# The last chunk of expert weights by halves of its output columns, in a one-core decoder layer with 32 experts

## What is computed

```python
h = h + mixed @ w_out
h = h + MoE(RMSNorm(h))      # top-4 of 32 experts, at most a few tokens each
output = RMSNorm(h)          # [1, 256, 1024] float32

# one expert, for the tokens that chose it
hu  = xb @ w_up[e] + b_up[e]                       # 1024 -> 2 x 1024
act = min(hu[:, :1024], 7) * sigmoid(1.702 * ...) * (clip(hu[:, 1024:], -7, 7) + 1)
y   = act @ w_down[e] + b_down[e]                  # 1024 -> 1024
# each token's outputs are weighted by its gates and added to its row of h
```

## Time and profile before

| | |
|---|---|
| time, median of 3 runs | 1242.39 us (1242.19 to 1242.48) |
| time of the profiled execution | 1243.28 us |
| its span, first to last instruction | 1241.6 us |
| TensorE busy | 1160.3 us, 93% |
| VectorE, ScalarE busy | 392.5 us (32%), 241.3 us (19%) |
| read from memory | 455.35 MB, 368 GB/s over the span |
| granted TensorE clock, mean | 0.982 |

### The profile page before, as it was taken

The page is one execution under the profiler, slowest core; times in us unless marked ns, Lnnn a source line. Parts: engine busy times, 40 slices in busy tenths (PEclk is TensorE's granted clock), DMA queues, the critical chain, the costliest instruction groups (busy, mean ns, idle before and its releaser), DMA issues.

```text
span 1241.6 us, 16246 instructions
## 1 busy us (share of the span) xinstructions
PE 1160.3 (93%) x6984; PEld 593.1 (48%) x6984; DVE 392.5 (32%) x670; ACT 241.3 (19%) x334; POOL 10.8 (1%) x29
## 2 busy tenths in 40 slices
PE   9999999999999999988898889989898988989997
PEld 8888887888633334333333333333333333333332
DVE  7765746666522112121111111112121112111112
ACT  5343445554401001010000000000000001000002
POOL 2000000000000000000000000000000000000000
PEclk9999999999999999999999999999999999999999
DMA  8744333496999999999999999999999999999996
GB/s 263 260 170 179 136 136 136 153 362 227 364 423 425 433 431 430 430 432 431 433 431 433 429 435 431 432 434 430 433 430 435 430 433 434 429 433 429 425 427 276
DMA packets 46429, 456.95 MB, mean 368 GB/s; under 512 B 5588, under 2 KB 5736, under 8 KB 31128
## 3 DMA queue, kind: packets, MB, share of 16 engines
q1 hardware_dynamic: 46088, 455.61, 88.2%
q10 hardware_dynamic: 304, 0.79, 0.2%
HBM read 455.35 MB, written 1.05 MB: 368 GB/s over the span
## 4 chain that ended last, share of the span: by engine, by line
PE 59%; DMA 36%; DVE 3%; ACT 1%; issue 0%; SPq 0%; DVEq 0%
PE ps L1410 57%; DMA ring<-in_w_up_dram 22%; DMA arena<-in_w_up_dram 10%; DMA ring<-in_w_down_dram 3%; DMA ring<-in_w_in_dram 1%; PE ps L1924 1%; DVE w_split L910 1%; ACT w_split L627 0%; PE ps L1815 0%; PE ps L1604 0%; DVE arena L955 0%; DVE arena L1077 0%; PE ps L1712 0%; DVE bias_p L954 0%; DVE arena L956 0%
## 5 line engine op out<-in xcount | busy, mean ns | idle before, releaser
L1410 PE MATMUL ps<-ring,arena 128*64 128x512 f32 x2304 | 521.4, 606 | 51.9 <-DMA ring<-in_w_up_dram 50.4
L1410 PEld LDWEIGHTS ps<-ring,arena 128*64 128x64 f32 x2304 | 163.5, 139 | 379.5 <-issue 301.0
L1410 PE MATMUL ps<-arena 128*64 128x512 f32 (+3 forms) x920 | 202.8, 563 | 18.2 <-DMA arena<-in_w_up_dram 17.3
L1329 DVE TENSOR_SCALAR arena<-ps 128x512 f32<-128x512 f32 x32 | 22.1, 692 | 487.1 <-PE ps L1410 487.1
L1410 PEld LDWEIGHTS ps<-arena 128*64 128x64 f32 (+1 forms) x920 | 77.9, 148 | 130.1 <-issue 99.5
L910 DVE TENSOR_TENSOR w_split<-ring,w_split 128x2048 fp32r<-128x2048 f32 x48 | 109.9, 2291 | 82.0 <-ACT w_split L627 81.8
L820 ACT ACTIVATE arena<-arena 128x512 f32<-128x512 f32 x32 | 20.2, 631 | 551.9 <-DVE arena L1329 551.9
L1410 PE MATMUL ps<-w_split,x_split 128*128 128x512 f32 x528 | 123.4, 392 | 1.0 <-DVE w_split L910 0.6
L627 ACT ACTIVATE w_split<-ring 128x2048 fp32r<-128x2048 f32 x47 | 89.8, 1914 | 111.4 <-PE ps L1410 95.7
L1410 PEld LDWEIGHTS ps<-w_split,x_split 128*128 128x128 f32 x528 | 98.4, 188 | 22.0 <-issue 1.2
L1410 PE MATMUL ps<-x_split,w_split 128*128 128x256 f32 (+1 forms) x544 | 93.0, 331 | 0.0
(11 more groups left out here) (245 smaller groups left out, 603.1 us busy)
## 6 DMA issues: line engine op xcount, KB each, us to landing
ring<-in_w_up_dram SPq DMA_DIRECT2D x38, 4096.0 KB, 31.1
ring<-in_w_down_dram SPq DMA_DIRECT2D x19, 4096.0 KB, 30.0
arena<-in_w_up_dram SPq DMA_DIRECT2D x12, 4096.0 KB, 31.1
ring<-in_w_up_dram SPq DMA_DIRECT2D x20, 2048.0 KB, 11.9
ring<-in_w_in_dram SPq DMA_DIRECT2D x17, 2048.0 KB, 7.9
arena<-in_w_down_dram SPq DMA_DIRECT2D x7, 4096.0 KB, 29.9
arena<-in_w_up_dram SPq DMA_DIRECT2D x8, 2048.0 KB, 15.8
ring<-in_w_down_dram SPq DMA_DIRECT2D x8, 2048.0 KB, 24.3
```

The lines of the kernel that those rows point to most:

```text
L1329: dve.tensor_scalar(glu_c, ps[bank][:, :], LIMIT, None, ALU.min).then_inc(glu_ok, 1)
L1410: return pe.matmul(dst, lhsT, rhs, start=start, stop=stop, skip_group_check=True)
```

## The change

It has four parts.

1. F is loaded by output columns: first columns 0 to 511 of all four rows (1 MB), then columns 512 to 1023 of rows 0 and 1, of row 2, and of row 3. The rows that are copied per partition are then 2 KB long each.
2. TensorE multiplies F half by half: four products for half 0, then k0 and k1 of half 1, then `last_share` of half 0, then k2 and k3 of half 1, then `last_share` of half 1. E is taken as two groups of rows, half 0 before half 1 in each. The two halves use two banks (`LAST_BANK`), and each is evicted to `y_last` by itself, 64 partitions by 512. The 31st expert's `scatter` moves from behind F to between E and F.
3. The final norm squares, weights and sums 128 x 512 pieces: four squares instead of two, the first columns' squares folded into a bias (`ssq`) for the square root, and all four output pieces are weighted by `lnf` first and scaled by the inverse root later.
4. U2, U3, G0 and G1 are loaded in two pieces of 1 MB each, and TensorE may begin on the first.

The pieces stand in the order of the engines: SyncE, ScalarE, VectorE, TensorE.

```diff
+                    at_once = 1 if u == 2 and c >= 2 else 2
+                    sp.dma_start(dst[:, 0:at_once, :], rows[:, 2 * (c % 2):2 * (c % 2) + at_once, :]).then_inc(landed, 16)
+                    if at_once == 1:
+                        sp.dma_start(dst[:, 1, :], rows[:, 2 * (c % 2) + 1, :]).then_inc(part_in[c - 2], 16)
...
+                        sp.dma_start(dst[:, 0:2, :], rows[:, 0:2, :]).then_inc(chunk_in[place], 16)
+                        sp.dma_start(dst[:, 2:4, :], rows[:, 2:4, :]).then_inc(part_in[2 + d], 16)
...
-                for lo, hi, landed in pieces:
-                    sp.dma_start(dst[:, lo:hi, :], rows[:, lo:hi, :]).then_inc(landed, 16)
-                if d:
-                    for half, landed in enumerate((last_part_in, last_half_in)):
-                        cols = slice(half * 512, half * 512 + 512)
-                        sp.dma_start(dst[:, 3, cols], rows[:, 3, cols]).then_inc(landed, 16)
...
+            sp.dma_start(dst[:, :, 0:512], rows[1, :, :, 0:512]).then_inc(early_in[3], 16)
+            sp.dma_start(dst[:, 0:2, 512:D], rows[1, :, 0:2, 512:D]).then_inc(chunk_in[PLACES - 1], 16)
+            sp.dma_start(dst[:, 2, 512:D], rows[1, :, 2, 512:D]).then_inc(last_part_in, 16)
+            sp.dma_start(dst[:, 3, 512:D], rows[1, :, 3, 512:D]).then_inc(last_half_in, 16)
...
-            act.activation(y_last[:, 0, :], ps[1][:, :], ACT.Copy, scale=g_slot[:, 1:2]).then_inc(y_out, 1)
+            def last_part(half):
+                rows = slice(half * CAP, half * CAP + CAP)
+                act.wait_ge(half_sum, half + 1)
+                act.activation(y_last[rows, 0, :], ps[LAST_BANK[half]][rows, :], ACT.Copy, scale=g_slot[rows, 1:2])\
+                   .then_inc(y_out, 1)
+            def last_square(t, half):
+                act.wait_ge(sum_ps, 2 * half + t + 1)
+                act.activation(at(t * D + half * 512, 512), ps[SUM_BANK[2 * t + half]][:, :], ACT.Square,
+                               accum_out=ssq4[:, t, half:half + 1]).then_inc(last_sq, 1)
...
+            last_part(0)
+            last_square(0, 0)
+            last_part(1)
+            act.wait_ge(scaled_ok, 1)
+            last_square(1, 0)
+            for t in range(TT):
+                if t:
+                    act.wait_ge(scaled_ok, 3)
+                last_square(t, 1)
+                act.wait_ge(part_ok, 2)
+                act.wait_ge(last_sq, 3 + t)
+                last_square_root(t)
...
+            last_low(0)
             dve.wait_ge(lnf_in, 16)
+            weighted(1, 0)
+            last_low(1)
+            dve.wait_ge(last_sq, 1)
+            weighted(0, 0)
+            dve.wait_ge(last_sq, 2)
+            dve.tensor_scalar(ssq[:, :], ssq4[:, :, 0], 1.0 / D, EPS, ALU.mult, ALU.add).then_inc(part_ok, 1)
+            weighted(1, 1)
+            dve.wait_ge(last_sq, 3)
+            weighted(0, 1)
             last_inverse(0)
+            out_half(0, 0)
             last_inverse(1)
+            out_half(0, 1)
+            out_half(1, 0)
...
+            for half in range(2):
+                last_down(0, half, (0, 1))
+            chunk_landed(last_turn, TURN_CHUNKS - DOWN_CHUNKS)
+            for half in range(2):
+                last_down(0, half, (2, 3))
             pe.wait_ge(y_ok, n_last(3))
             pe.wait_ge(selT_ok, n_last(4))
             for t in range(TT):
                 for piece in range(2):
                     scatter(0, t, piece)
-            pe.wait_ge(y_out, n_last(4))
+            pe.wait_ge(early_in[3], 16)
+            last_down(1, 0, range(4)).then_inc(half_sum, 1)
+            pe.wait_ge(chunk_in[PLACES - 1], 64)
+            last_down(1, 1, (0, 1))
             pe.wait_ge(selT_ok, n_last(5))
-            for t in range(TT):
-                last_share(0, t)
             pe.wait_ge(y_ok, n_last(4))
             for t in range(TT):
-                last_share(1, t)
+                for piece in range(2):
+                    last_share(piece, t, 0)
+            pe.wait_ge(last_part_in, 16)
+            last_down(1, 1, (2,))
+            pe.wait_ge(last_half_in, 16)
+            last_down(1, 1, (3,)).then_inc(half_sum, 1)
+            pe.wait_ge(y_out, n_last(4) + 1)
+            for t in range(TT):
+                last_share(0, t, 1)
+            pe.wait_ge(y_ok, n_last(4) + 1)
+            for t in range(TT):
+                last_share(1, t, 1)
```

More of the change, by code:

```diff
@@ L235, in layer @@
             sem(n) for n in ("last_part_in", "last_half_in", "ln1_in", "ln1_ps", "xs_ok", "glr_split_ok"))
-        first_half_in = [sem(f"first_half_in{c}") for c in range(DENSE_RING)]
+        part_in = [sem(f"part_in{c}") for c in range(DENSE_RING + 2)]
         vec_in, glr_in, bias_in, router_in, glaw_in, lnf_in = (
@@ L533, in _ @@
             end = TURN_CHUNKS - DOWN_CHUNKS
             sp.wait_ge(chunk_used, last_turn * TURN_CHUNKS + (end - PLACES + 1))
[L535 to L546 removed]
+            rows = w_down[0, E - 1, :, :].rearrange("(p d s) n -> d p s n", d=DOWN_CHUNKS, s=4)
@@ new lines, in _ @@
+            dst = chunk_at[PLACES - 2].rearrange("p (s n) -> p s n", s=4)
+            sp.dma_start(dst[:, 0:2, :], rows[0, :, 0:2, :]).then_inc(early_in[2], 16)
+            sp.dma_start(dst[:, 2:4, :], rows[0, :, 2:4, :]).then_inc(chunk_in[PLACES - 2], 16)
+            sp.wait_ge(chunk_used, last_turn * TURN_CHUNKS + (end + 1 - PLACES + 1))
+            dst = chunk_at[PLACES - 1].rearrange("p (s n) -> p s n", s=4)
+            sp.dma_start(dst[:, :, 0:512], rows[1, :, :, 0:512]).then_inc(early_in[3], 16)
@@ L1890, in first_down, with down @@
                     ins.then_inc(chunk_used, 1)
-            def down(i, u, last, bank=3, source=None, between=None, late=False, parts=False):
-                first = down_end(u, last) - DOWN_CHUNKS
-                hidden = (actT if source is None else source).rearrange("p (k s) -> p k s", k=4)
+            def down(i, u, between=None, late=False, parts=False):
+                first, bank = down_end(u, False) - DOWN_CHUNKS, 3
+                hidden = actT.rearrange("p (k s) -> p k s", k=4)
                 bias(bank, u, 2 * D)
                 pe.wait_ge(actT_ok, i * UNROLL + (u + 1))
-                if not last:
-                    chunk_landed(i, first)
+                chunk_landed(i, first)
                 for d in range(DOWN_CHUNKS):
@@ L1977, in expert_pe @@
                 else:
-                    down(i, u, False, late=bool(late), parts=by_chunk and u > 1)
+                    down(i, u, late=bool(late), parts=by_chunk and u > 1)
             pe.wait_ge(xin_half_ok, 1)
@@ L2014, in down_between @@
                     one_hot_transposed(last_turn * (TT * UNROLL) + TT * UNROLL, 0)
-            down(last_turn, UNROLL - 2, False, between=down_between, late=True)
-            down(last_turn, UNROLL - 1, True, bank=1, source=act_last)
+            down(last_turn, UNROLL - 2, between=down_between, late=True)
+            pe.wait_ge(actT_ok, n_last(4))
+            for half in range(2):
+                last_bias(half)
+            pe.wait_ge(early_in[2], 16)
+            for half in range(2):
+                last_down(0, half, (0, 1))
+            chunk_landed(last_turn, TURN_CHUNKS - DOWN_CHUNKS)
+            for half in range(2):
+                last_down(0, half, (2, 3))
             pe.wait_ge(y_ok, n_last(3))
```

113 lines of the change are left out of this document (59 added, 54 removed).

## The result

The changed kernel takes **1249.39 us**, the median of six runs (1247.68 to 1251.63), beside 1242.43 for the kernel before on the same chip; the ratio is 1.0051, with a 95% interval of 1.0040 to 1.0062. It is slower by half a per cent. The profiled execution took 1248.15 us with a span of 1246.4, so 4.8 us more than the span of 1241.6 before. The forecast was 1247.1 (1244.5 to 1249.2), and for the profiled execution 1248.0 with a span near 1246.3. The profiled execution fits to 0.2 us; the median lies 2.3 above the forecast and 0.2 above the range.

A forecast was written before the change was run, and what follows sets the result against it. TensorE and transfers bound the kernel in turn; what counts is the last bytes' landing and the work behind. F's products 5.45 us later, the way behind 0.8 shorter: span 4.7 us more, 1248.0 profiled, median 1247.1 (1244.5 to 1249.2).

The forecast's parts named there:

- Pace of one half of the array, 0.43 us per record: TensorE in F: each array half keeps its own pace, 0.86 us per product, so an unpaired product leaves the other half empty.
- Rival 2: TensorE in F: a lone array half runs faster, perhaps 0.215 us per record; 1244.5 us, chance 0.10.
- Pieces, 0.3: Weight stream: splitting U2, U3, G0, G1 (0.24 us) and F's 2 KB rows make everything later by 0.3 us.
- rival 1: TensorE in E: the array looks only one record ahead, so E ends 1.4 us later; 1248.4 or 1248.5, chance 0.25.
- takes its records as they come: TensorE in E: each array half runs its records without regard to the other, so the new order costs nothing.
- Five changes of form, up to 0.2 each: TensorE behind E: five changes of tiling mode, before once, may each drain the engine, up to 0.2 us each.
- The added wait, 1.58, at full price for 64 partitions: Before half 0's shares: TensorE waits for eviction and residue, taking 1.58 us, the same as for 128 partitions.
- Rival 3: ScalarE and VectorE behind F: evictions of 64 partitions at half price, 1.4 us less; 1245.7, chance 0.05.
- Shares, k2 and k3, T: TensorE behind the wait: half-0 shares 1.20 us, k2 and k3 alone 1.88; all products end at T = 1237.9.
- T to the end, 0.8 given back: Products' end (T) to span end: 8.35 us instead of 9.15, from halved squares and work done early.
- Rival 4: TensorE behind the standstill: clock falls to 1.2 GHz, shares and k2, k3 take twice as long; 1250.3, chance 0.05.
- the median of the runs is 0.9 lower: Last step: from the profiled execution's 1248.0 to the median of the runs, 0.9 us less, giving 1247.1.

The follow-up runs named there:

- e6: e1 with F's products interleaved (half 0 k0, k1, half 1 k0, half 0 k2, half 1 k1, half 0 k3, then half 1 k2, k3): 1245.46 us.
- e7: Changed kernel with the 31st expert's shares moved from ahead of F to behind k0, k1 of half 1, into TensorE's standstill: 1247.61 us.
- e3: Kernel before with only U2, U3, G0 and G1 loaded and waited for in two 1 MB pieces: 1242.79 us, ratio 1.0001.
- e1: Changed kernel with k2, k3 of half 1 ahead of half 0's shares and their wait, and both evictions ahead of the squares: 1245.90 us.
- e8: Changed kernel with VectorE scaling and storing output piece (0,0) before it weights piece (0,1): 1248.21 us.
- e5: The changed kernel itself, unaltered, run and profiled again: 1248.53 us, ratio 1.0040.
- e2: Changed kernel with nine small products, without use for the result, filling TensorE's two standstills: 1247.69 us, ratio 1.0042.
- e10: Kernel before with F loaded by columns and multiplied in e6's order, everything behind F whole: 1244.27 us, ratio 1.0012.
- e9: e6 with the 31st expert's shares moved behind F's products: 1245.27 us, ratio 1.0018.

## Why the prediction was right, and where it was not

**The loss, taken apart.** From the kernel before to the changed one in steps of one thing each, by the tails: F by columns, with half 1's bytes behind half 0's, in e6's order, 14.07 - 12.80 = **1.27**; all behind F by halves, 15.10 - 14.07 = **1.03**; the 31st's shares ahead of F, in e6's order, 15.02 - 15.10 = **-0.08**; all of half 0 ahead of half 1, 15.40 - 15.02 = **0.38**; half 0's shares and their wait ahead of k2 and k3, 17.67 - 15.40 = **2.27**. Together 4.87. Half of the loss is the new order of TensorE's work, as forecast; in that order the shares ahead of F cost 0.40 (e7), in e6's they cost nothing.

**Point by point.**

- *Pace of one half of the array, 0.43 us per record.* Right. The four lone records took 1.93 us for 1.88 forecast. Rival 2 falls.
- *Pieces, 0.3.* Not decided: e3's median is 0.25 above, within its noise. F's last piece landed at 1231.28 in both profiles, which is partly luck, since landings move by up to 1.4 us between executions. This and E's end, 1228.14 instead of 1228.55, made F start at 1229.21 instead of 1229.8.
- *E, and rival 1.* E's sixteen records went in two groups of 1.94, without a stagger; rival 1's 5.8 us did not come. But "takes its records as they come" was wrong as well. In E three records of half 0 are still to start when half 1 starts; in F half 1 starts only when three are left. The row of F before proved one; I weighed one against all, and it is three. In the changed kernel this costs almost nothing, since k0 and k1 of half 1 end 0.06 us behind half 0; it cost my expectation of e1 0.5 us. Rival 1's price was wrong too: 13 steps is what strict program order would take. If one record may be passed, each group of E takes six steps for four, and E would end some 0.9 us later, not 1.4.
- *Five changes of form, up to 0.2 each.* They cost nothing that shows: where nothing else held it, the first product of the new form starts 0.07 us before the modelled end of the last of the old (1228.08, 1229.21, 1235.65).
- *The added wait, 1.58, at full price for 64 partitions.* Right: 0.68 and 0.74, standstill 1.65. Rival 3 falls.
- *Shares, k2 and k3, T.* 1.16 for 1.20; T at 1237.6 for 1237.9.
- *T to the end, 0.8 given back.* Mis-sized: 0.27 (1237.58 to 1246.42 is 8.84, and 1232.45 to 1241.56 was 9.11). My steps hold up to the last store, which is issued at T + 5.2 for 5.35 forecast. But I added 3.0 for the store to the end, and it took 3.6. In eleven of twelve profiles the span ends 4.49 to 4.54 us behind the **first** store, while it ends 2.9 to 3.7 behind the last: four stores issued closer together end no sooner. What counts is T to the first store, 4.6 before and 4.3 now. e8, whose first store came 0.3 earlier without a gain, speaks against the first store alone as the measure.
- *Rival 4, the clock.* I gave it 0.05 and let it apply to all executions or none. e8's profile shows it, at 1.42 us. With standstills open, 1249 us and more was taken by 4 of 6 runs of the changed kernel (one of them 1251.63), 3 of 8 in e5 and 2 of 10 in e8; with them filled, by none of 12 in e7, and in e2 only by the run that lost its time earlier. The mean granted clock parts these 24 runs without an overlap: 0.978 to 0.980 in the nine at 1249 us and more, 0.981 to 0.983 in the fifteen others. That this fall is what lifts the median of the first six runs from near 1248 to 1249.4 is inferred from these counts and one profile; a profile of the unaltered changed kernel with the fall was not caught.

The sum was right to 0.1 us in the profiled execution with some luck: F started 0.6 earlier than forecast, which left 0.35 at T, and the way from T was 0.5 longer. The step that failed for the median is the one that took the profiled execution for all, "the median of the runs is 0.9 lower": it was 1.24 higher than the profiled execution (1249.39 against 1248.15). A profile of a kernel is one draw of its runs, and the distance to the median of the kernel before does not carry over.

No version that loads F by columns beats the kernel before: the best, e10, is 1.5 us slower.

## What to carry to other kernels

Splitting an output for an earlier first half pays only if the second half's operands are not pushed back by it: here the halves shared one TensorE and one stream, so the early half was bought with the late one, and the late one sets the end. An eviction or residue on half the partitions took as long as on all (0.68 and 0.74 us against 0.69 and 0.75), so two halves are double that work on the engines behind. Before a wait is put into TensorE's queue, look at what stands behind it and whether its operands are already there; work that waits for nothing belongs into the gap (e7), and the counts of long runs speak for it on account of the clock as well.

## What was not expected of the hardware

- TensorE started a product of the other half of the array past three waiting records of the first, not past more: 1.77 us behind the first of eight in one block (the profiles of the changed kernel, e1, e2, e5, e7 and e8), within 0.05 us of its landing with one or two waiting (e6, e9, e10), and 0.01 us behind the first of four (E).
- The granted clock fell to 0.5 behind a standstill of 1.65 us in one execution (e8) and not in two of the changed kernel, whose TensorE program is the same up to there (tails 19.15, and 17.67 twice), and at 327 us in two profiles of twelve (e2, e10), where F's first piece landed 3.4 to 5.3 us later than in the others.
- The stores of the output, 1.05 MB in all, moved at some 385 GB/s and took 2.9 us from the first packet to the last whenever they were issued close together, and the end stood 4.5 us behind the issue of the first.
